# Seven products that nobody reads taken out of TensorE's queue, at the entry of the second mixer and in the routing

## What is computed

```python
for l in range(DEPTH):
    mod = (c_act @ w_ada[l] + b_ada[l])[:, None, :]
    shift1, scale1, gate1, shift2, scale2, gate2 = jnp.split(mod, 6, axis=-1)
    h = x * (1 + scale1) + shift1
    y = hybrid_mixer(h, ...)
    x = layer_norm(DEEPNORM_ALPHA * x + gate1 * y, ln1_g[l], ln1_b[l])
    h = x * (1 + scale2) + shift2
    f = swiglu(h, ...) if l % 2 == 0 else top2_moe(h, router_w, router_b, wg, wu, wd)
    x = layer_norm(DEEPNORM_ALPHA * x + gate2 * f, ln2_g[l], ln2_b[l])

def top2_moe(h, router_w, router_b, wg, wu, wd):
    logits = t @ router_w + router_b
    top_v, top_i = lax.top_k(logits, TOP_K)
    gates = jax.nn.softmax(top_v, axis=-1)
    for e in range(N_EXPERTS):
        out = out + combine[:, e:e + 1] * swiglu(t, wg[e], wu[e], wd[e])
```

## Time and profile before

| | us |
|---|---|
| median of three runs | 1418.47 |
| lowest, highest | 1417.40, 1418.54 |
| the profiled execution | 1417.46 |
| its span | 1415.7 |
| TensorE busy | 1390.7 |
| VectorE busy | 1251.7 |
| ScalarE busy | 1012.6 |
| mean granted clock | 0.994 |

### The profile page before, as it was taken

The page is one execution under the profiler, slowest core; times in us unless marked ns, Lnnn a source line. Parts: engine busy times, 40 slices in busy tenths (PEclk is TensorE's granted clock), DMA queues, the critical chain, the costliest instruction groups (busy, mean ns, idle before and its releaser), DMA issues.

```text
span 1415.7 us, 20150 instructions
## 1 busy us (share of the span) xinstructions
PE 1390.7 (98%) x7013; PEld 1149.1 (81%) x7013; DVE 1251.7 (88%) x1388; ACT 1012.6 (72%) x1286; POOL 63.3 (4%) x123
## 2 busy tenths in 40 slices
PE   6999999999999999999999999999999999999996
PEld 4876999997967888888888888888888888888885
DVE  5987888876799989998998899999889899899998
ACT  2453544454355888888988888888898888888884
POOL 1000000000013500000000000000000000001000
PEclk9999999999999999999999999999999999999998
DMA  9996398977564999999999999999999999999970
GB/s 361 416 412 240 143 349 290 378 282 276 207 258 171 385 369 366 392 380 375 379 393 365 366 398 367 380 383 387 367 379 392 365 371 392 387 362 390 413 306 32
DMA packets 203472, 482.16 MB, mean 341 GB/s; under 512 B 6944, under 2 KB 31630, under 8 KB 203418
## 3 DMA queue, kind: packets, MB, share of 16 engines
q1 hardware_dynamic: 198848, 470.31, 88.1%
q0 software_dynamic: 1584, 5.77, 1.0%
q10 hardware_dynamic: 2986, 5.38, 1.0%
HBM read 475.67 MB, written 5.77 MB: 340 GB/s over the span
## 4 chain that ended last, share of the span: by engine, by line
PE 96%; DVE 2%; DMA 1%; ACT 0%; issue 0%; POOL 0%; SPq 0%; ACTq 0%; DVEq 0%; POOLq 0%
PE ps L1794 27%; PE ps L1796 27%; PE ps L1795 27%; PE ps L1957 2%; PE ps L2144 2%; PE ps L1815 2%; PE ps L1918 2%; PE ps L1971 1%; PE ps L1756 1%; DMA raw<-in_w_ada_dram 1%; PE ps L1731 1%; PE ps L1867 0%; PE ps L2094 0%; PE ps L1773 0%; PE ps L1729 0%; PE ps L1898 0%
## 5 line engine op out<-in xcount | busy, mean ns | idle before, releaser
L1424 DVE TENSOR_TENSOR low<-raw,w_hi 128x1024 fp32r<-128x1024 f32 x448 | 531.6, 1218 | 24.4 <-ACT w_hi L853 16.2
L853 ACT ACTIVATE w_hi<-raw 128x1024 fp32r<-128x1024 f32 x448 | 470.2, 1061 | 84.3 <-PE ps L1796 79.4
L1795 PE MATMUL ps<-low,h_hi 128*128 128x512 f32 x904 | 351.9, 389 | 0.0
L1794 PE MATMUL ps<-w_hi,h_lo 128*128 128x512 f32 x680 | 269.5, 396 | 0.0
L1796 PE MATMUL ps<-w_hi,h_hi 128*128 128x512 f32 x680 | 265.3, 390 | 0.0
L1795 PE MATMUL ps<-low,hid_hi 128*128 128x512 f32 x528 | 205.7, 390 | 0.0
L1795 PEld LDWEIGHTS ps<-low,h_hi 128*128 128x128 f32 x904 | 169.9, 188 | 34.2
L1424 DVE TENSOR_TENSOR low<-raw,e_hi 128x1024 fp32r<-128x1024 f32 x112 | 136.7, 1220 | 19.8 <-ACT e_hi L853 19.8
L1796 PEld LDWEIGHTS ps<-w_hi,h_hi 128*128 128x128 f32 x680 | 127.6, 188 | 27.4
L1794 PEld LDWEIGHTS ps<-w_hi,h_lo 128*128 128x128 f32 x680 | 127.8, 188 | 24.9
L1424 DVE TENSOR_TENSOR low<-raw,hx_lo 128x1024 fp32r<-128x1024 f32 x112 | 136.5, 1219 | 3.7
(11 more groups left out here) (377 smaller groups left out, 2268.0 us busy)
## 6 DMA issues: line engine op xcount, KB each, us to landing
raw<-in_moe_w_gate_dram SPq DMA_DIRECT2D x56, 2048.0 KB, 8.5
raw<-in_moe_w_up_dram SPq DMA_DIRECT2D x56, 2048.0 KB, 8.6
raw<-in_moe_w_down_dram SPq DMA_DIRECT2D x56, 2048.0 KB, 8.7
raw<-in_w_ada_dram SPq DMA_DIRECT2D x20, 2048.0 KB, 12.7
raw<-in_w_in_dram SPq DMA_DIRECT2D x6, 2048.0 KB, 12.5
raw<-in_ffn_w_gate_dram SPq DMA_DIRECT2D x11, 1024.0 KB, 8.3
raw<-in_ffn_w_up_dram SPq DMA_DIRECT2D x11, 1024.0 KB, 10.9
raw<-in_ffn_w_down_dram SPq DMA_DIRECT2D x11, 1024.0 KB, 4.9
```

Source lines behind the costliest of these rows:

```text
L853: act.activation(e_hi[k % ERING], raw[moe_slot(m)][:, (k % 4) * UNIT:(k % 4 + 1) * UNIT], ACT.Copy).then_inc(unit_hi, 1)
L1424: dve.tensor_tensor(low[moe_slot(m)][:, part], raw[moe_slot(m)][:, part], e_hi[k % ERING].bitcast(F32), ALU.subtract).then_inc(unit_lo, 1)
L1794: pe.matmul(o, x_lo, hi, start=first, stop=False, skip_group_check=True)
L1795: pe.matmul(o, x_hi, lo, start=False, stop=False, skip_group_check=True)
```

## The change

The four calls of `warm` are taken out: two products ahead of the second mixer's first transposes, one between the halves of the last gate, three after the logits, one after the place products. With each call its wait for the gate goes too. The function stays, without a caller; `unread` at the start of the program is untouched. Nothing that another engine waits for is changed, and nothing that is computed.

```diff
             def mixer(l):
                 if l >= 1:
-                    warm(2, 2, 1)
                     turn_input(2, 0)
...
                 if t == 1:
                     ada(1, 5, 0)
-                    warm(1, 1, 1)
                     ada(1, 5, 1)
                     turn_input(3, 1)
...
             m.then_inc(logit_mm, 1)
 
-            warm(3, 1, 1)
             pe.wait_ge(chosen_ready, 1)
...
             pe.matmul(ps[:, 0, 64 + 2 * E:64 + 3 * E], ones[:, :], chosen[:, 1, :], start=False, stop=True).then_inc(place_mm, 1)
-            warm(1, 1, 1)
-
             def gather(i):
```

## The result

The changed kernel takes 1421.87 us at the median of eight executions (1420.47 to 1422.23), the kernel before 1418.47 us (1417.40 to 1418.55). The ratio is 1.0026, with an interval of 1.0017 to 1.0036. So the change costs 3.4 us. The forecast was 1421.6 us. In what follows a cold stretch is one in which the granted clock is 0.50, and a fall is its beginning.

A forecast was written before the change was run, and what follows sets the result against it. TensorE was taken to bound the kernel, with delays before the fully busy expert loop never caught up. From 1418.0 us, 1.2 + 2.4 - 0.05 = +3.6 us for routing gave 1421.6 us, range 1418.8 to 1424.8.

The forecast's parts named there:

- Direct gain nothing: At the four removed calls: the next work waits for other engines, so direct terms sum to -0.1 to 0 us.
- part 4: Before the first gather: removing one product lets the gather start 0 to 0.1 us sooner, taken as 0.05 us.
- One fall in routing, between 440 and 443.4: In routing, before the chosen experts are counted: the clock falls once, costing +3.6 us, bounds +1.3 to +6.3; chance 0.60.
- rival B: Second or longer cold stretch, in the passage (+1.4 to +2.85) or before the router's second half (+2.3): 1423.8 us; chance 0.25.
- Term (a): Place products, lines 2067 to 2071: ten passes take twice their 1.1 us, +1.1 us, and +0.1 for the last's end.
- Term (b): From the gather on: half the work in a cold stretch of recovery is lost, +2.4 us, bounds 1.4 to 2.85.
- Term (c): At the router: its 16 passes, 2.3 us, would double if the clock fell before 437.9, +2.3 us.
- The passage, "no fall" with 3 to 1: Into the second mixer: the clock holds, odds 3 to 1; a fall would cost +1.4 to +2.85 us.
- The base: Starting time of the kernel before: 1418.0 us, between its profiled 1417.46 and its median 1418.47.
- the sum 3.6: Total for routing: 1.2 + 2.4 - 0.05 = +3.6 us, bounds +1.3 and +6.3.
- The transposes: In the passage: if transposes don't count as busy, 3.5 us hold no counting work and a fall is likelier than not.
- Rival D: At the removed calls: the unread passes delay the next products, so up to 6.0 us come back, 1412.0; chance 0.04.

The follow-up runs named there:

- e9_all: The changed kernel measured again, all seven unread products removed from the kernel before: 1422.60 us, ratio 1.0021 to 1.0046.
- e8_keep_three: Kernel before with only the three products after the logits kept; passage, gate and gather lose theirs: 1421.45 us, ratio 1.0015 to 1.0035.
- e1_passage: Kernel before without the two products ahead of the second mixer's first transposes, the other five kept: 1420.08 us, ratio 1.0011 to 1.0029.
- e5_gate: Kernel before without the one product between the halves of the last gate: 1418.59 us, ratio 0.9998 to 1.0017.
- e11_before: The kernel before once more, nothing taken out: 1418.15 us, ratio 0.9993 to 1.0011.
- e10_gate_last: Kernel before without the product between the gate's halves and the one ahead of the gather: 1421.56 us, ratio 1.0018 to 1.0037.
- e6_last: Kernel before without the one product ahead of the first gather: 1418.77 us, ratio 0.9998 to 1.0017.
- e4_five: Kernel before with five products instead of three after the logits: 1419.43 us, ratio 1.0003 to 1.0021.

## Why the prediction was right, and where not

- **Direct gain nothing: right.** All four idle times are ended by the releasers named. The 0.05 us of part 4 was wrong: in the changed kernel the gather starts 446.28, 0.15 us after the selection matrix (445.65 + 0.48), just as with the unread passes ahead of it; nothing came back.
- **One fall in routing, between 440 and 443.4: right in the profiled execution,** at 440.5, and without the three after the logits at 442.4. It isn't right for every execution: that of e9_all falls at 434.6, which the forecast gave to rival B, and six of the first eight have a lower mean clock than the profiled one.
- **Term (a), +1.1 +0.1: right**, 1.01 us measured.
- **Term (b), +2.4: right**, 2.12 us measured. In the execution that stays cold until 455.1 the term is larger (gather to loop 448.98 to 455.91, 6.93 us for 4.01: +2.9), just above the upper bound of 2.85. The term was worked out from one recovery of 5.7 us; at the start of the changed kernel's execution the clock came back 2.9 us after the wide products had begun (24.53 to 27.5), and in its gather after 4.4 us (446.28 to 450.7). So its closeness is luck in part.
- **Term (c), +2.3, left to rival B: the size right, its make-up not.** The router's 16 passes did not double, they took 1.2 us more in e9_all; the gate's second half and the transposes, which the forecast left out, took 1.4 us more (438.81 - 435.24 against 437.53 - 435.36). Together +2.6 us.
- **The passage, "no fall" with 3 to 1: not borne out.** The profiled execution of the changed kernel has none, and neither have those of e9_all and e8_keep_three; but the profiles of e1_passage and of the thin products show a fall at 333.3 and 333.0. So it fell in two of five profiles without wide products there, and how often it does over many executions is open. The price was put at +1.4 to +2.85 and is 1.30 us.
- **The base.** The forecast had the kernel before as free of the effect at 1418.0. Its executions, from 1416.6 to 1418.8, contain it in about one of three. So total and range were right with two errors of opposite sign: most executions of the changed kernel lose more than one such fall costs, and the kernel before falls too. That the sum 3.6 meets the measured 3.4 is partly luck; the second measurement gave 5.0.
- **The transposes.** The Trainium skill (TensorE: Matmul & The Clock Gate, Part 4: PE-mode transpose) would have made a fall in the passage the rule. The runs show it in some executions and not in others; no run takes the transposes away, so whether they count stays open. That transposes don't run at the full clock, the traces contradict: eight take 1.04 us at 1.00 (changed kernel, 436.32) and 1.91 us at 0.50 (e9_all, 437.10).
- **Rival D, the cover in the way,** is out at full clock (the three starts keep their distance to their releasers without the cover) and true at half clock: 1.3 to 1.5 us of delay of the place products in the profiles of e1_passage, e5_gate, e8_keep_three and e11_before.

## What to carry to other kernels

That nobody waits for a product doesn't make it free to remove: ask for how long TensorE is without wide work if it goes, and look at the granted clock, not at the busy share. Cover must be wide and must end when the awaited engine is done: here 2.6 us in a hole of 2.85. With less the clock falls more often or for longer, more stands in the path, and at half clock even the fitting cover is too long. Take more than one profile before calling a stretch cold or not; one execution shows one of several cases.

## What the runs showed of the hardware that was not expected

- The same program falls at different places in different executions: the kernel before has 1.00 throughout its routing in one profile and 0.50 for 3.4 us in another. Its first cold stretch, too, begins at 22.84 us in one and 20.44 in the other (20.65 in the changed kernel). The windows of the three, and of e1_passage, in which it begins at 22.73:

```profile
22.00:23.00 1.00, 1.00 (x11) 0.92 1.03 401
20.00:21.00 1.00, 0.58 (x5) 0.72 1.04 409
20.00:21.00 1.00, 0.68 (x7) 0.82 1.05 413
22.00:23.00 1.00, 1.00 (x10) 0.86 1.03 401
```

- Measured from where this first cold stretch begins, the later falls lie at fixed distances. The first fall in routing comes 419.8 us later in nine of the twelve profiles that have one (440.48 - 20.65 in the changed kernel, 440.28 - 20.44 in e11_before, 442.57 - 22.73 in e1_passage, where the work itself comes 1.3 us late after its cold passage). In e9_all and e10_gate_last it comes 413.0 us later, in e6_last 423.3. Both falls in the passage come 310.6 us later (333.34 - 22.73, 333.03 - 22.42); in the three profiles without one the same distance ends at 331.3 to 332.2, ahead of the transposes. So in these profiles the place of the first cold stretch tells where a later fall can lie, and it differs from execution to execution by 2.4 us (20.44 to 22.84), enough to put thin or wide work ahead of it. In the kernels that keep their wide passes after the logits, TensorE had been at these passes for 1.8 to 2.2 us at 419.8 us in the profiles that stayed at 1.00 there (the kernel before at 442.68, e4_five, e6_last), and for 0.3 to 1.2 us in those that fell (e11_before, e1_passage, e5_gate, e8_keep_three). All this was read from the profiles afterwards; no run moved the wide passes to test it.
- A gather of 32 passes of 128 columns does not always bring the clock back: 6.72 us at 1.2 GHz in one execution, with TensorE busy throughout, while in another the clock returned after 2.0 us of it, with a wide product ahead of it.
- Passes of one or eight columns take twice as long at half clock as well (eight columns: 0.43 us for two instead of 0.22).
